# Expert weights in blocks of 896 columns, with a twelve-slot ring and h turned on VectorE

## The chip, the cores and the metric

The kernel runs on one core of one Trainium2 chip. The metric is device time in microseconds for one execution, as the median of several runs. One further execution was recorded by the hardware profiler; the rows below come from it.

## What is computed

One step of a two-layer decoder trunk with model width 1024, for 256 prompt tokens and 8 sample tokens (T = 264), all in 32-bit floats. Layer 0 is an HGRN2 recurrence and a dense SwiGLU, layer 1 a gated short convolution and a mixture of eight experts, of which each token takes two. The change touches the experts alone:

```python
def swiglu(x, w1, w3, w2):
    return (jax.nn.silu(x @ w1) * (x @ w3)) @ w2

def moe_swiglu(x, router, w1, w3, w2):
    logits = (xt @ router).astype(F32)
    top_v, top_i = lax.top_k(logits, TOP_K)
    gates = jax.nn.softmax(top_v, axis=-1)
    ...
    for e in range(N_EXPERTS):
        out = out + combine[:, e:e + 1] * swiglu(xt, w1[e], w3[e], w2[e])
```

w1 and w3 of an expert are 1024 x 3584, w2 is 3584 x 1024. The three together are 44.04 MB per expert and 352.3 MB for the eight.

## The kernel before

**Rows.** The tokens of an expert are gathered into at most 96 rows (`SLOT`), which are three groups of 32 (`GROUPS`, `GROUP`). POOL scatters the normed tokens to `xg_rows` in HBM with indirect DMAs. For each later expert SP loads 96 rows into `xg`, PE turns them (`turn_rows`, L2451), ACT copies them to `xgt` (L1064). The expert's result y is built up in PSUM (`Q[1]`, banks 0 and 1), copied by ACT to `ybuf` and stored to `y_rows`. For the last expert y stays on the chip. Near the end POOL gathers the results of the other experts from `y_rows` (L675).

**Blocks of h.** The 3584 columns of h are worked in FB = 7 blocks of 512. A block has three parts. `up_m(0)` forms x @ w1 of the block, `up_m(1)` forms x @ w3, and `down_m` multiplies h by 512 rows of w2 and adds to y. The stationary operand always is 128 x 32, and four such operands stand side by side in the array, one for each 32 partitions of the output. In `up_m` three of them (L2438) hold the three groups of tokens and see 384 columns (`MAIN`); the fourth (L2442) takes the three groups in turn with the last 128 columns (`TAIL`). In `down_m` the moving operand is 256 columns of w2 for all four (L2500, L2503). Each 32-bit matmul is recorded as two instructions, each with its own weight load.

**Turning h.** ACT forms silu(x @ w1) as `hs` (L1078), DVE multiplies by x @ w3 into `hx` (L1840). Tokens are then on partitions, and `down_m` needs the columns of h there. PE therefore transposes `hx` in three 128 x 128 matmuls (`turn`, L2482) into bank 2 of `Q[0]`, and ACT copies them to `ht` (L1092).

**Order on PE.** One pass of the inner loop is: `up_m(0)` of block i+1, `turn` of block i, `up_m(1)` of block i+1, `down_m` of block i. After six passes the last block of the expert is turned, the rows of the next expert are turned, the last `down_m` runs, both `up_m` of the next expert's first block run, and `clear_y` (L2459, tiny matmuls that start a new y) follows. These stand behind the inner loop as a second copy of the code. The loop over experts goes round seven times, and the last expert has code of its own.

**Loading.** The weights come in pieces of 1 MB (`pair`, `load_piece`, L457): four K tiles of 512 columns of w1 or w3, in rows of 2 KB, or two tiles of w2, in rows of 4 KB. There are 42 pieces per expert and a ring of RING = 6 slots. SP issues the load of a piece when PE has counted (`used`) the piece six places earlier as done. Six pieces are loaded ahead (`early_piece`), the last of them when the normed rows are finished, as its slot holds `gffn` until then.

**Other buffers.** In the stages before the experts, raw weights go to `raw` (three slots of 16 KB a partition) and their split parts to `whi` and `wlo`.

Of the kernel before, what the change touches and what calls it, by code (L numbers as in the profile page):

```python
# [24 lines left out]
P = 128  # L25
# [4 lines left out]
RING = 6  # L30
SLOT = 96
GROUP = 32
MAIN = 384
TAIL = P
# [3 lines left out]
def build(nc, x_prompt, x_sample, state_hgrn, state_conv, norm_mix, norm_ffn, norm_final,  # L38
# [28 lines left out]
    JOB = 3 * FB  # L67
    SLOTS = 3 * SLOT
    GROUPS = SLOT // GROUP
    PIECES = 2 * JOB  # L70
# [3 lines left out]
    assert PIECES % RING == 0 and C_FFN * 2 + 4 == 24 and FW == MAIN + TAIL and D == 4 * YW  # L74
# [4 lines left out]
    with ExitStack() as ctx:  # L79
# [83 lines left out]
        for g_ in range(2):  # L163
# [30 lines left out]
            R0, ("xs", [P, TT, D], F32), ("xgt", [P, DT, SLOT], F32), ("hx", [P, MAIN], F32),  # L194
            ("ht", [P, GROUPS, P], F32), ("sqx", [P, DT, T], F32))
        sqx_at = o - size([P, DT, T], F32)
        (xg, hs), _ = region(sqx_at, ("xg", [P, D], F32), ("hs", [P, MAIN], F32))
# [8 lines left out]
        (ring,), o = region(RING_AT, ("ring", [P, RING, PW], F32))  # L206
        (gffn,), _ = region(RING_AT + (RING - 1) * size([P, PW], F32), ("gffn", [P, D], F32))
# [7 lines left out]
            raw_at + size([P, RAW, CW], F32), ("ht_last", [P, GROUPS, P], F32), ("yh", [P, D], F32R),  # L215
            ("yl", [P, D], F32R), ("pick", [P, T], F32R))
        assert o <= xT_at
# [72 lines left out]
        piece_loaded = [sem(f"piece_loaded{i}") for i in range(RING)]  # L290
        hi_done, lo_done, used = sem("hi_done"), sem("lo_done"), sem("pieces_used")

        OBANK = (0, 1, 3)

# [56 lines left out]
        def _(sp):  # L351
# [102 lines left out]
            def load_piece(q, src):  # L454

                slot = q % RING
                sp.dma_start(ring[:, slot, :].rearrange("p (k w) -> p k w", k=src.shape[1]), src  # L457
                             ).then_inc(piece_loaded[slot], 16)

            def early_piece(q):  # L460

                w = (moe_w1, moe_w1, moe_w3, moe_w3, moe_w1, moe_w1)[q]
                cols = slice(FW, 2 * FW) if q >= 4 else slice(0, FW)
                load_piece(q, tiles_of(w, 0, 4 * (q % 2), 4)[:, :, cols])
# [31 lines left out]
            def head(k, e, row):  # L496

                if not isinstance(k, int):
                    rows_in(k, row)
                    pair(k, 0, tiles_of(moe_w1, e, 0, DT)[:, :, 0:FW])  # L500
                    pair(k, 2, tiles_of(moe_w3, e, 0, DT)[:, :, 0:FW])
                    pair(k, 4, tiles_of(moe_w1, e, 0, DT)[:, :, FW:2 * FW])

            def body(k, e, row, ahead):

                with sp.Fori(0, FB - 2) as i:
                    pair(k, 6, tiles_of(moe_w3, e, 0, DT)[:, :, bass.ds(i * FW + FW, FW)], i)
                    pair(k, 8, tiles_of(moe_w2, e, i * 4, 4), i)
                    pair(k, 10, tiles_of(moe_w1, e, 0, DT)[:, :, bass.ds(i * FW + 2 * FW, FW)], i)
                q = 6 * (FB - 1)  # L510
                if ahead:
                    rows_in(k + 1, row + SLOTS)
                pair(k, q, tiles_of(moe_w3, e, 0, DT)[:, :, FW * (FB - 1):FW * FB])
                pair(k, q + 2, tiles_of(moe_w2, e, 4 * (FB - 2), 4))
                pair(k, q + 4, tiles_of(moe_w2, e, 4 * (FB - 1), 4))
                if ahead:
                    pair(k, q + 6, tiles_of(moe_w1, e + 1, 0, DT)[:, :, 0:FW])
                    pair(k, q + 8, tiles_of(moe_w3, e + 1, 0, DT)[:, :, 0:FW])
                    pair(k, q + 10, tiles_of(moe_w1, e + 1, 0, DT)[:, :, FW:2 * FW])
# [184 lines left out]
        def _(act):  # L704
# [355 lines left out]
            def gathered(k):  # L1060

                act.wait_ge(sem("xg_turned"), k + 2)
                act.wait_ge(used, k * PIECES + (M0 - 4))
# [11 lines left out]
            def silu(nth, last):  # L1075
                act.wait_ge(used, last)
                act.wait_ge(sem("hx_ready"), nth + 1)
                a.activation(hs[:, :], Q[0][:, 0, 0:MAIN], ACT.Silu).then_inc(sem("hs_ready"), 1)  # L1078

            def head(k, e, row):  # L1080
                if not isinstance(k, int):
                    gathered(k)
                silu(k * FB, k * PIECES + (M0 + 2))

            def body(k, e, row, ahead):
                pk = k * PIECES + M0
                kb = k * FB
# [14 lines left out]
                silu(kb + (i + 1), pk + (i * 6 + 6))  # L1102
                turned(kb + i, pk + (i * 6 + 4))
                if ahead:
                    turned(kb + (FB - 1), pk + (6 * FB - 2))
                    gathered(k + 1)
                else:
                    if isinstance(k, int):
# [1489 lines left out]
```

## Time and profile before

| | us |
|---|---|
| median of 3 runs | 1491.7 |
| lowest and highest run | 1490.43, 1495.47 |
| the profiled execution | 1485.0 |
| its span on the core | 1483.2 |
| PE busy in the span | 1453.7 |
| DVE busy, ACT busy | 432.6, 325.1 |
| read from HBM, written | 445.53 MB, 29.66 MB |

The span is the time from the first to the last recorded instruction. Matmuls overlap one another, so the time that PE needs for a piece of work is read from the distance between the starts of matmuls and not from their durations. The experts begin at 541.8 us of the span and their last matmul ends at about 1468 us.

### The profile page before, as it was taken

To read this page: it belongs to the slowest core of one execution; us is meant where nothing else is said; L and a number is where in the kernel's file an instruction comes from. 1 tells how busy PE (TensorE), PEld (TensorE's weight loads), DVE (VectorE), ACT (ScalarE), POOL (GpSimd) and SP (SyncE) were. 2 spreads that over 40 slices of the span, in tenths; PEclk is the share of its full clock that TensorE was granted. 3 is DMA by queue.
4 is the path that set the end of the run, shared out by engine and by line. 5 is a ranking of instruction groups with operands and counts; after the bars stand their busy time and mean duration, and the time that the engine had idled before them with its cause. 6 is when DMAs were issued, how large, how long until landed. Compare 5 with 4: busy or idle time off the path is not lost.

```text
span 1483.2 us, 45976 instructions
## 1 busy us (share of the span) xinstructions
PE 1453.7 (98%) x20875; PEld 1384.1 (93%) x20876; DVE 432.6 (29%) x508; ACT 325.1 (22%) x381; POOL 69.5 (5%) x65
## 2 busy tenths in 40 slices
PE   9998999999999999999999999999999999999996
PEld 8988899999999989999999999999999999999894
DVE  6898866565677620000000000000000000000004
ACT  5644353433353320010010010001001001001012
POOL 1035200000000020000000000000000000001000
PEclk9999999999999999999999999999999999999998
DMA  8645686777648149999999999999999999999994
GB/s 310 220 130 177 221 310 245 268 269 270 232 152 316 40 164 396 392 376 394 396 374 395 394 376 395 393 378 394 394 378 392 396 378 393 394 377 397 388 393 184
DMA packets 214033, 475.95 MB, mean 321 GB/s; under 512 B 8811, under 2 KB 26315, under 8 KB 213981
## 3 DMA queue, kind: packets, MB, share of 16 engines
q1 hardware_dynamic: 210536, 466.47, 86.1%
q10 hardware_dynamic: 2164, 4.40, 0.8%
q0 software_dynamic: 1280, 4.33, 0.8%
q8 instruction: 40, 0.66, 0.2%
q14 instruction: 13, 0.10, 0.0%
HBM read 445.53 MB, written 29.66 MB: 320 GB/s over the span
## 4 chain that ended last, share of the span: by engine, by line
PE 86%; DMA 1%; DVE 1%; ACT 0%; issue 0%; DVEq 0%; SPq 0%
PE Q L2442 25%; PE Q L2438 15%; PE Q L2500 13%; PE Q L1981 8%; PE Q L1982 8%; PE Q L1983 8%; PE Q L2503 7%; PE Q L2482 2%; DMA ring<-in_moe_w 1%; PE Q L2415 0%; PE Q L2451 0%; PE Q L2341 0%; PE Q L2459 0%; PE Q L2369 0%; ACT yrows L1149 0%
## 5 line engine op out<-in xcount | busy, mean ns | idle before, releaser
L2442 PE MATMUL Q<-ring,xgt 128*32 128x128 f32 x5376 | 605.3, 273 | 0.0
L2438 PE MATMUL Q<-ring,xgt 128*32 128x384 f32 x5376 | 597.9, 487 | 0.0
L2442 PEld LDWEIGHTS Q<-ring,xgt 128*32 128x32 f32 x5376 | 582.2, 110 | 0.0
L1981 PE MATMUL Q<-xh,whi 128*128 128x264 f32 x1024 | 294.3, 287 | 5.5 <-DVEq L1285 1.8
L2500 PE MATMUL Q<-ring,ht 128*32 128x256 f32 x3960 | 295.2, 379 | 2.7 <-DMA ring<-in_moe_w 2.2
L2503 PE MATMUL Q<-ring,ht 128*32 128x256 f32 x1320 | 294.5, 379 | 0.0
L1982 PE MATMUL Q<-xl,whi 128*128 128x264 f32 x1024 | 291.7, 285 | 0.0
L1983 PE MATMUL Q<-xh,wlo 128*128 128x264 f32 x1024 | 290.3, 284 | 0.0
L1840 DVE TENSOR_TENSOR hx<-hs,Q 128x384 f32<-128x384 f32 x56 | 31.1, 554 | 883.0 <-PE Q L2442 883.0
L2438 PEld LDWEIGHTS Q<-ring,xgt 128*32 128x32 f32 x5376 | 215.1, 109 | 10.4 <-issue 8.1
L1981 PEld LDWEIGHTS Q<-xh,whi 128*128 128x128 f32 x1024 | 193.3, 189 | 8.2 <-issue 4.2
L1174 DVE TENSOR_TENSOR wlo<-raw,whi 128x2048 fp32r<-128x2048 f32 x77 | 175.8, 2295 | 75.1 <-ACT whi L952 59.5
L1982 PEld LDWEIGHTS Q<-xl,whi 128*128 128x128 f32 x1024 | 193.4, 189 | 0.3
L1983 PEld LDWEIGHTS Q<-xh,wlo 128*128 128x128 f32 x1024 | 193.1, 189 | 0.0
L2500 PEld LDWEIGHTS Q<-ring,ht 128*32 128x32 f32 x3960 | 162.8, 110 | 26.4 <-issue 4.0
L1078 ACT ACTIVATE hs<-Q 128x384 f32<-128x384 f32 x56 | 27.5, 491 | 716.8 <-PE Q L2442 716.8
L2503 PEld LDWEIGHTS Q<-ring,ht 128*32 128x32 f32 x1320 | 144.3, 110 | 0.0
L715 ACT ACTIVATE whi<-raw 128x2048 fp32r<-128x2048 f32 x41 | 78.2, 1912 | 72.0 <-PE Q L1983 71.0
L952 ACT ACTIVATE whi<-raw 128x2048 fp32r<-128x2048 f32 x36 | 68.8, 1911 | 90.2 <-PE Q L1983 90.2
L1983 PE MATMUL Q<-fh,wlo 128*128 128x264 f32 x192 | 54.9, 286 | 0.0
L1982 PE MATMUL Q<-fl,whi 128*128 128x264 f32 x192 | 54.6, 285 | 0.0
L1981 PE MATMUL Q<-fh,whi 128*128 128x264 f32 x192 | 54.4, 283 | 0.0
(282 smaller groups left out, 837.3 us busy)
## 6 DMA issues: line engine op xcount, KB each, us to landing
ring<-in_moe_w SPq DMA_DIRECT2D x336, 1024.0 KB, 9.4
raw<-in_ffn_w SPq DMA_DIRECT2D x42, 1024.0 KB, 6.3
raw<-in_hgrn_w_in SPq DMA_DIRECT2D x16, 1024.0 KB, 6.1
raw<-in_conv_w_in SPq DMA_DIRECT2D x12, 1024.0 KB, 5.8
xg_rows<-zeros SPq DMA_DIRECT2D x6, 1536.0 KB, 9.5
y_rows<-zeros SPq DMA_DIRECT2D x6, 1536.0 KB, 9.6
raw<-in_hgrn_w_out SPq DMA_DIRECT2D x4, 1024.0 KB, 5.1
raw<-in_conv_w_out SPq DMA_DIRECT2D x4, 1024.0 KB, 5.5
```

The source lines that it names most:

```text
L715: a.activation(whi[:, buf, :], raw[:, slot, PW * half:PW * (half + 1)], ACT.Copy).then_inc(hi_done, 1)
L952: a.activation(whi[:, base % SPLIT, :], raw[:, n % RAW, PW * (base % 2):PW * (base % 2 + 1)], ACT.Copy).then_inc(hi_done, 1)
L1174: v.tensor_tensor(low, raw[:, slot, PW * half:PW * (half + 1)], high.bitcast(F32), ALU.subtract).then_inc(lo_done, 1)
L1840: v.tensor_tensor(hx[:, :], hs[:, :], Q[0][:, 1, 0:MAIN], ALU.mult).then_inc(sem("hx_ready"), 1)
L1981: t_.matmul(out, w[wslice], xhi, start=start, stop=False, **kw)
L1982: t_.matmul(out, w[wslice], xlo, start=False, stop=False, **kw)
L1983: return t_.matmul(out, lo[wslice], xhi, start=False, stop=stop, **kw)
L2438: t_.matmul(out[g_, 0:MAIN], xgt[:, kt, g_], w[:, FW * c:FW * c + MAIN], start=(kt == 0), stop=(kt == DT - 1), skip_group_check=True)
L2442: mm = t_.matmul(out[SLOT:P, TAIL * n:TAIL * (n + 1)], xgt[:, kt, g_], w[:, FW * c + MAIN:FW * (c + 1)], start=(kt == 0 and n == 0), stop= ...
L2482: mm = t_.transpose(Q[0][:, 2, P * c:P * (c + 1)], hx[:, P * c:P * (c + 1)], ident[:, :])
L2500: mm = t_.matmul(Q[1][GROUP * n:GROUP * (n + 1), bank, col:col + YW], rows_of_h(ht, f, n), w[:, D * c + YW * cb:D * c + YW * (cb + 1)], st ...
L2503: mm = t_.matmul(Q[1][SLOT:P, bank, col:col + YW], rows_of_h(ht, f, cb), w[:, D * c + 3 * YW:D * (c + 1)], start=False, stop=(last and f = ...
```

## The change

The 3584 columns are worked in MB = 4 blocks of MW = 896. In `up_m` every group of tokens is multiplied by all four column groups at once: four matmuls of HW = 224 columns, one for each 32 partitions of the output. The 224 columns are every fourth run of 32 columns of the block, seven runs 512 bytes apart (`columns`). x @ w1 takes banks 0 and 1 of `Q[0]`, x @ w3 banks 2 and 3. With this layout a transpose of each 32 x 32 block, by one DVE instruction, puts the columns of h on partitions as `down_m` needs them. PE's `turn` and ACT's copy are gone.

The pieces of w1 and w3 are two K tiles of 896 columns (0.875 MB, rows of 3.5 KB), those of w2 two tiles of 128 rows (1 MB), the fourth of a block one tile (0.5 MB): 48 pieces per expert. The ring has twelve slots. Five are where the old ring was, six lie in `raw` and one at the end of `wlo`; the latter seven are loaded when the convolution's output projection is done with that memory. `gffn` has a place of its own.

The code behind the inner loop is gone: the next expert's first `up_m` pair is the last pass of the loop, and `clear_y`, `turn_rows` and one wait stand in the loop under conditions. The diff is cut; of removed lines only some are shown.

```diff
-RING = 6
+RING = 12
+RING_LOW = 5
 SLOT = 96
 GROUP = 32
-MAIN = 384
-TAIL = P
+MW = 896
+HW = MW // 4
...
-        (ring,), o = region(RING_AT, ("ring", [P, RING, PW], F32))
-        (gffn,), _ = region(RING_AT + (RING - 1) * size([P, PW], F32), ("gffn", [P, D], F32))
+        (ring_low, gffn), o = region(RING_AT, ("ring_low", [P, RING_LOW, PW], F32), ("gffn", [P, D], F32))
+        (ring_mid,), o = region(raw_at, ("ring_mid", [P, 2 * RAW, PW], F32))
+        (ring_top,), o = region(xT_at - size([P, PW], F32), ("ring_top", [P, PW], F32))
+        assert RING == RING_LOW + 2 * RAW + 1
...
+        piece_loaded += [raw_loaded[i // 2][i % 2] for i in range(2 * RAW)] + [sem(f"piece_loaded{RING_LOW}")]
+        loaded_before = [C_MOE // RAW if RING_LOW <= i < RING_LOW + 2 * RAW else 0 for i in range(RING)]
...
+        def h_part(which):
+
+            return Q[0][:, 2 * which:2 * which + 2, :].rearrange("p b (h n) -> p (b h) n", n=YW)[:, 0:GROUPS, 0:HW]
...
-            sp.wait_ge(sem("xs_gained"), TT)
-            sp.wait_ge(sem("xs_ready"), TT)
-            early_piece(5)
-
-            def pair(k, q, src, reg=None):
-
-                for half in range(2):
-                    free = k * PIECES + (2 * C_MOE + q + half - RING + 1)
-                    sp.wait_ge(used, free if reg is None else free + reg * 6)
-                    n = src.shape[1] // 2
-                    load_piece(q + half, src[:, n * half:n * (half + 1), :])
+            for i in range(2 * RAW):
+                if i % 2 == 0:
+                    sp.wait_ge(lo_done, 2 * (C_MOE - RAW + i // 2 + 1))
+                early_piece(RING_LOW + i)
+            sp.wait_ge(used, 2 * C_MOE)
+            early_piece(RING - 1)
+
+            def four(k, q, src, reg=None):
+
+                for j in range(4):
+                    free = k * PIECES + (2 * C_MOE + q + j - RING + 1)
+                    sp.wait_ge(used, free if reg is None else free + reg * RING)
+                    load_piece(q + j, src[:, 2 * j:min(2 * j + 2, src.shape[1]), :])
 
...
+                with sp.Fori(0, MB - 2) as i:
+                    four(k, 12, tiles_of(moe_w3, e, 0, DT)[:, :, bass.ds(i * MW + MW, MW)], i)
+                    four(k, 16, tiles_of(moe_w2, e, i * MT, MT), i)
+                    four(k, 20, tiles_of(moe_w1, e, 0, DT)[:, :, bass.ds(i * MW + 2 * MW, MW)], i)
+                q = RING * (MB - 1)
                 if ahead:
                     rows_in(k + 1, row + SLOTS)
+                four(k, q, tiles_of(moe_w3, e, 0, DT)[:, :, MW * (MB - 1):MW * MB])
+                four(k, q + 4, tiles_of(moe_w2, e, MT * (MB - 2), MT))
                 if ahead:
+                    four(k, q + 8, tiles_of(moe_w1, e + 1, 0, DT)[:, :, 0:MW])
+                    four(k, q + 12, tiles_of(moe_w3, e + 1, 0, DT)[:, :, 0:MW])
+                    four(k, q + 16, tiles_of(moe_w2, e, MT * (MB - 1), MT))
+                    four(k, q + 20, tiles_of(moe_w1, e + 1, 0, DT)[:, :, MW:2 * MW])
+                else:
+                    four(k, q + 8, tiles_of(moe_w2, e, MT * (MB - 1), MT))
...
-                def turned(nth, w2_used, ht=ht):
-                    act.wait_ge(sem("h_turned"), nth + 1)
-                    act.wait_ge(used, w2_used)
-                    a.activation(ht[:, :, :].rearrange("p a s -> p (a s)"), Q[0][:, 2, 0:MAIN], ACT.Copy
-                                 ).then_inc(sem("ht_ready"), 1)
-
-                with act.Fori(0, FB - 2) as i:
-                    silu(kb + i + 1, pk + i * 6 + 6)
-                    turned(kb + i, pk + i * 6 + 4)
-                i = FB - 2
...
+            def mul(nth, last, down_before, ht=ht):
                 dve.wait_ge(used, last)
                 dve.wait_ge(sem("hs_ready"), nth + 1)
+                if not isinstance(nth, int) or nth:
+                    dve.wait_ge(sem("ht_ready"), nth)
+                v.tensor_tensor(hx[:, :].rearrange("p (g n) -> p g n", n=HW),
+                                hs[:, :].rearrange("p (g n) -> p g n", n=HW), h_part(1), ALU.mult
                                 ).then_inc(sem("hx_ready"), 1)
+                dve.wait_ge(sem("hx_ready"), nth + 2)
+                if down_before is not None:
+                    dve.wait_ge(used, down_before)
+                v.transpose(ht[:, :], hx[:, :]).then_inc(sem("ht_ready"), 1)
 
...
+            def columns(w, c, n):
+
+                return w[:, MW * c:MW * (c + 1)].rearrange("p (a j r) -> p j a r", j=4, r=GROUP)[:, n, :, :]
+
+            def up_m(which, k, q, reg, first=False):
+
+                for kt in range(DT):
+                    if kt % 2 == 0:
+                        w = piece(k, q + kt // 2, reg)
+                    if first and kt % 4 == 0:
+                        pe.wait_ge(sem("xgt_ready"), kt // 4 + 1)
+                    for g_ in range(GROUPS):
+                        bank, col = 2 * which + g_ // 2, YW * (g_ % 2)
+                        for n in range(4):
+                            mm = t_.matmul(Q[0][GROUP * n:GROUP * (n + 1), bank, col:col + HW],
+                                           xgt[:, kt, GROUP * g_:GROUP * (g_ + 1)], columns(w, kt % 2, n),
+                                           start=(kt == 0 and g_ % 2 == 0), stop=(kt == DT - 1),
+                                           skip_group_check=True)
+                    if kt % 2 == 1:
+                        mm.then_inc(used, 1)
 
...
-                def turn(nth):
-                    pe.wait_ge(sem("hx_ready"), nth + 2)
-
-                    for c in range(GROUPS):
-                        mm = t_.transpose(Q[0][:, 2, P * c:P * (c + 1)], hx[:, P * c:P * (c + 1)],
-                                          ident[:, :])
-                    mm.then_inc(sem("h_turned"), 1)
-
...
+                def down_tile(w, f, cb, last, ht):
+
+                    c = f % 2
+                    bank, col = cb // 2, YW * (cb % 2)
+                    for n in range(GROUPS):
+                        t_.matmul(Q[1][GROUP * n:GROUP * (n + 1), bank, col:col + YW],
+                                  rows_of_h(ht, f, n), w[:, D * c + YW * cb:D * c + YW * (cb + 1)],
+                                  start=False, stop=(last and f == MT - 1), skip_group_check=True)
+                    return t_.matmul(Q[1][SLOT:P, bank, col:col + YW], rows_of_h(ht, f, cb),
+                                     w[:, D * c + 3 * YW:D * (c + 1)],
+                                     start=False, stop=(last and f == MT - 1), skip_group_check=True)
+
...
+                with pe.Fori(0, MB if ahead else MB - 1) as i:
+                    if ahead:
+                        again_if_ahead(i)
                     pe.wait_ge(sem("hs_ready"), kb + i + 1)
+                    up_m(0, k, 8, i)
+                    with pe.If(i == 0):
+                        clear_y(k)
+                    pe.end_ifs()
+                    pe.wait_ge(sem("hx_ready"), kb + i + 2)
+                    up_m(1, k, 12, i)
+                    if ahead:
+                        with pe.If(i == MB - 2):
+                            turn_rows(k + 1)
+                        pe.end_ifs()
+                    down_m(kb + i, 16, i, False)
+                if ahead:
+                    return
```

## Rows read from the trace of the kernel before

**Rows 1.** The page: busy time of PE, and GB/s moved in forty equal slices.
```profile
PE 1453.7 (98%) x20875; PEld 1384.1 (93%) x20876; DVE 432.6 (29%) x508; ACT 325.1 (22%) x381; POOL 69.5 (5%) x65
...
GB/s 310 220 130 177 221 310 245 268 269 270 232 152 316 40 164 396 392 376 394 396 374 395 394 376 395 393 378 394 394 378 392 396 378 393 394 377 397 388 393 184
```

**Rows 2.** Chain that ended last, in order of time: start us, us, what.
```profile
882.02 0.66 PE Q L2451 x8
...
1228.25 0.66 PE Q L2451 x8
...
1267.04 0.48 PE Q L2482 x3
...
1343.66 0.66 PE Q L2451 x8
...
1385.26 0.48 PE Q L2482 x3
```

**Rows 3.** Timeline of PE, one block: start us, us, line, tiles, count.
```profile
904.46 0.55 PE L2482 MATMUL Q<-ident,hx 128*128 128x128 f32 x3
904.94 0.52 PE L2438 MATMUL Q<-ring,xgt 128*32 128x384 f32 x3
...
910.12 0.39 PE L2500 MATMUL Q<-ring,ht 128*32 128x256 f32 x3
...
915.30 0.50 PE L2438 MATMUL Q<-ring,xgt 128*32 128x384 f32 x3
...
920.74 0.55 PE L2482 MATMUL Q<-ident,hx 128*128 128x128 f32 x3
```

**Rows 4.** Timeline of PE at the end of one expert.
```profile
996.88 0.55 PE L2482 MATMUL Q<-ident,hx 128*128 128x128 f32 x3
997.26 0.83 PE L2451 MATMUL Q<-ident,xg 96*128 96x96 f32 x8
998.17 0.42 PE L2500 MATMUL Q<-ring,ht 128*32 128x256 f32 x3
...
1013.96 0.60 PE L2459 MATMUL Q<-ident 32*128 32x1 f32 x4
1014.49 0.52 PE L2438 MATMUL Q<-ring,xgt 128*32 128x384 f32 x3
```

**Rows 5.** Waits of PE: for whom, us in total, times, longest.
```profile
PE Q L2500 <- DMA ring<-in_moe_w: 2.2, 2, 1.8
```

**Rows 6.** Timeline of PE in layer 0, four column groups with 128 columns each.
```profile
115.34 1.08 PE L2084 MATMUL Q<-U,z 128*32 128x128 f32 x32
```

**Rows 7.** Groups by line from 560 to 1460 us: busy us, mean ns of one.
```profile
L1840 DVE TENSOR_TENSOR hx<-hs,Q 128x384 f32<-128x384 f32 x55 | 30.5, 554 | 870.2 <-PE Q L2442 870.2
L1830 DVE SCALAR_TENSOR_TENSOR xs<-xs,tk,xr 128x1024 f32<-128x1024 f32 x2 | 2.6, 1282 | 0.0
```
```profile
L1064 ACT ACTIVATE xgt<-Q 128x768 f32<-128x768 f32 x7 | 5.7, 811 | 1.3 <-PE Q L2451 1.3
```

**Rows 8.** Busy time in stretches; the last three columns are clock, DMA share, GB/s.
```profile
705.00:710.10 5.10, 5.10 (x91) 4.73 (x87) 0.00 (x0) 0.92 (x2) 0.00 (x0) 1.00 1.03 402
...
710.20:715.60 5.40, 5.40 (x107) 5.30 (x103) 0.55 (x1) 0.00 (x0) 0.00 (x0) 1.00 1.05 387
...
900.10:916.40 16.30, 16.30 (x300) 15.79 (x296) 0.56 (x1) 0.91 (x2) 0.00 (x0) 1.00 1.04 394
```

**Rows 9.** Loads at L457 issued in 550 to 560, 1240 to 1250, 1360 to 1370.
```profile
DMA to landing us min/median/max: 9.6/10.2/10.2
```
```profile
DMA to landing us min/median/max: 9.6/10.2/10.3
```
```profile
DMA to landing us min/median/max: 15.5/16.0/16.6
```

**Rows 10.** The page: the queue of instruction loads, and the loads of the ring.
```profile
q8 instruction: 40, 0.66, 0.2%
...
ring<-in_moe_w SPq DMA_DIRECT2D x336, 1024.0 KB, 9.4
```

More of the change, by code:

```diff
@@ L73, in build @@
     CIN_ORDER = [2, 3, 4, 5, 0, 1]
[L74 removed]
+    assert MB * MW == moe_w1.shape[3] and RING == DT + (MT + 1) // 2 and HW <= YW and D == 4 * YW
+    assert C_FFN * 2 + 4 == 24 and C_MOE % RAW == 0
     def kp(w):
@@ L456, in load_piece @@
                 slot = q % RING
[L457 removed]
+                n, w = src.shape[1], src.shape[2]
+                sp.dma_start(ring_slot(slot)[:, 0:n * w].rearrange("p (k w) -> p k w", k=n), src
                              ).then_inc(piece_loaded[slot], 16)
             def early_piece(q):
[L462 to L464 removed]
+                w = (moe_w1, moe_w3, moe_w1)[q // 4]
+                cols = slice(MW, 2 * MW) if q >= 8 else slice(0, MW)
+                load_piece(q, tiles_of(w, 0, 2 * (q % 4), 2)[:, :, cols])
             for c in range(6):
@@ L1135, in body @@
                 act.dma_start(y_rows[bass.ds(row, SLOT), :], ybuf[0:SLOT, :]).then_inc(sem("y_stored"), 16)
-                if ahead:
-                    silu(kb + FB, pk + (6 * FB + 2))
-                else:
+                if not ahead:
                     act.wait_ge(sem("y_stored"), k * 16 + 32)
@@ L2515, in body @@
-                kb = k * FB
-                ends = isinstance(k, int) and not ahead
-                with pe.Fori(0, FB - 2 if ends else FB - 1) as i:
-                    pe.wait_ge(sem("hs_ready"), kb + i + 1)
-                    up_m(0, k, 4, i)
-                    turn(kb + i)
-                    up_m(1, k, 6, i)
-                    down_m(kb + i, 8, i, False)
-                q = 6 * FB - 8
+                def rows_of_h(ht, f, n):
+                    return ht[:, HW * n + GROUP * f:HW * n + GROUP * (f + 1)]
@@ new lines, in down_m @@
+                def down_m(nth, q, reg, last, ends=False, ht=ht):
+                    pe.wait_ge(sem("ht_ready"), nth + 1)
+                    for f in range(4 if ends else MT):
+                        if f % 2 == 0:
+                            w = piece(k, q + f // 2, reg)
+                        for cb in range(GROUPS):
+                            mm = down_tile(w, f, cb, last, ht)
+                        if f % 2 == 1 or f == MT - 1:
+                            mm.then_inc(used, 1)
+                    if ends:
+                        ws = [piece(k, q + j, reg) for j in (2, 3)]
+                        for cb in range(GROUPS):
+                            for f in range(4, MT):
+                                mm = down_tile(ws[f // 2 - 2], f, cb, last, ht)
+                            if cb >= 1:
+                                mm.then_inc(sem("y_mm"), 1)
+                        pe.sem_inc(used, 2)
@@ L2532, in body @@
                         r = rows[t]
-                        mm = t_.transpose(Q[0][:, 3, P * t:P * t + r], pm[0:r, t, :], ident[0:r, 0:r])
+                        mm = t_.transpose(Q[1][:, 3, P * t:P * t + r], pm[0:r, t, :], ident[0:r, 0:r])
                     mm.then_inc(sem("rank_mm"), 1)
-                    down_m(kb + (FB - 2), q + 4, None, False, between=lambda: turn(kb + (FB - 1)))
-                    down_m(kb + (FB - 1), q + 6, None, True, True, None, ht_last)
-                    return
-                turn(kb + (FB - 1))
-                if ahead:
-                    turn_rows(k + 1)
-                down_m(kb + (FB - 1), q + 6, None, True)
-                if ahead:
-                    pe.wait_ge(sem("hs_ready"), kb + FB)
-                    pe.wait_ge(sem("xgt_ready"), k + 3)
-                    up_m(0, k, q + 8, None)
-                    up_m(1, k, q + 10, None)
-                    clear_y(k + 1)
+                down_m(kb + (MB - 1), RING * MB - 4, None, True, ends, ht_last if ends else ht)
             def finish(again):
```

146 lines of the change are left out of this document (49 added, 97 removed).

## The prediction

> **What bounds the kernel now.** I read the page first. PE is busy 98% of the span, and from the fifteenth slice on, where the experts run, the DMA engines move 376 to 397 GB/s in every slice [rows 1]. So two resources look full there, and the question is which of them sets the pace.
>
> The chain of waits says PE: it stays on PE almost everywhere, and consecutive experts follow at the same distance. From 882.02 to 1228.25 us are three experts of 115.41 us each [rows 2]. The one exception is in the last expert. From L2451 of one expert to the second L2482 of the next it is 1267.04 - 1228.25 = 38.79 us, and one expert later, to the turn that stands at the same place, 1385.26 - 1343.66 = 41.60 us [rows 2]. The 2.8 us more are a wait for weights; the waits of PE count 2.2 us of it at L2500 [rows 5].
>
> The timeline of one pass of the inner loop then shows what PE does [rows 3]. The second `up_m` takes 910.12 - 904.94 = 5.18 us, `down_m` 915.30 - 910.12 = 5.18 us, the next `up_m` with the switch to the transposes 920.74 - 915.30 = 5.44 us, and the transposes 904.94 - 904.46 = 0.48 us. Together 16.28 us, of which 0.74 us (0.26 for the change of shape and 0.48) exist only because PE turns h. There is no gap at 915.30, where the loop jumps back.
>
> The DMA is just behind. In a stretch in which mostly 4 KB rows land it moves 402 GB/s, in one of 2 KB rows 387, and over one whole pass 394, always with a DMA share above 1 [rows 8]. A pass needs 6.29 MB, so it costs the DMA 6.29 / 394 = 15.97 us, 0.3 us less than PE takes. The time from issue to landing is 10.2 us at the start of the first expert and again 10.2 us in the seventh [rows 9]. So the DMA never runs dry, and over a whole expert, with the rows loaded and stored, it takes about the same 115.4 us as PE.
>
> **What the ring tolerates.** With six slots a piece is issued when its slot is freed and needed five pieces later: 5 x 115.41 / 42 = 13.7 us. In the last expert, when POOL's gather shares the DMA, landing takes up to 16.6 us [rows 9]. 16.6 - 13.7 = 2.9 us, which is the wait found above. I use the same arithmetic for the new ring.
>
> **The change, part by part.**
>
> *PE's transposes go.* Seven experts lose six turns of 0.74 us in the loop and one at their end, next to `turn_rows`, which still changes the shape; that one costs 997.26 - 996.88 = 0.38 us [rows 4]. 7 x (6 x 0.74 + 0.38) = 33.7 us. The last expert loses seven at 0.74: 5.2 us. Sum -38.9 us, all on the path that sets the end. `turn_rows` (998.17 - 997.26 = 0.91 us) and `clear_y` (0.53 us) stay once per expert and only change place [rows 4].
>
> *The matmuls.* A K tile of 512 columns now takes 5.18 / 8 = 0.648 us, with six matmuls or twelve recorded instructions. 384 columns in half of that is 0.84 ns a column. 256 columns in `down_m` take 5.18 / 24 = 0.216 us, again 0.84 ns a column [rows 3]. Time goes with the columns. Four concurrent matmuls of 224 should then take 0.189 us, a K tile of 896 columns six of these, 1.135 us, and an expert 4 x (96 x 0.189 + 42 x 0.216) = 108.8 us, as now (7 x 15.54 = 108.8). Cost 0. But the instructions come denser. Now there are 96 matmul instructions in 5.18 us, 54 ns for each with its weight load. The change wants one per 1.135 / 24 = 47 ns. No stretch of the experts shows that. Layer 0 does, with the same four column groups in turn: 32 instructions at L2084 last 1.08 us with the last one's 0.27, so 26 ns each [rows 6]. The price is bounded by 0 there and by 54 ns in the experts: 24 x 54 = 1.296 us per K tile, +0.16 us x 512 K tiles = +82 us. I take 0, since L2084 is the nearer form, 32 columns of weights and short runs. The moving operand in runs of 32 columns, 512 bytes apart, is in no row; between 0 and the same +82 us, I take 0.
>
> The Trainium skill (TensorE: Matmul & The Clock Gate, section "Wait — 56ns, not 53.3ns?") says that with hardware decode off the sequencer spends about 62 ns per matmul. By it a K tile would take 24 x 62 = 1.49 us and the kernel would be some 140 us slower in the end; but the 54 ns in [rows 3] and the 26 ns in [rows 6] are both under it, so the trace disagrees.
>
> *DVE and ACT.* The multiply of 384 elements takes 554 ns and one of 1024 takes 1282 ns [rows 7], so 672 take about 0.86 us. The 32 by 32 transpose is not in the trace. It is bounded by nothing below and by two passes over a 1024-element row above, 2.6 us. I take 0.9 us. Either is hidden: the transpose may start when the earlier `down_m` ends, and its result is wanted after both `up_m` of the next block, 18 us later. DVE has nothing else queued but the next multiply. ACT's silu grows to about 0.75 us by the copy of 768 elements in 0.81 [rows 7] and has 9 us; it loses the copy to `ht`. In the last expert `ht_last` is filled 9 us before use. Cost 0.
>
> *The loop.* The jump back shows no gap today [rows 3]. Three conditions per pass are new; if the sequencer runs ahead as it does at the jump, they cost 0. The other bound: the instruction queue loaded 40 packets in 0.2% of 16 engines' span [rows 10], 0.002 x 16 x 1483 / 40 = 1.2 us each. I take 0.
>
> *The DMA.* 512 rows of 2 KB take 1.048 / 387 = 2.71 us, 5.29 ns a row. The 4 KB pieces get the rest of the pass: (15.97 - 4 x 2.71) / 2 = 2.565 us, 10.02 ns a row. A row of 3.5 KB on that line is 10.02 - 4.73 / 4 = 8.84 ns, and a piece of 256 rows 2.263 us. An expert costs 32 x 2.263 + 28 half-MB tiles x 1.283 = 108.3 us, and the row traffic 115.41 - 7 x 15.97 = 3.6 us more, 111.9 us. PE will need 115.41 - 4.82 = 110.6 us. So the DMA becomes the slower of the two, by 1.3 us an expert.
>
> *The ring* decides whether that shows. Twelve slots give 11 x 110.6 / 48 = 25.3 us instead of 13.7. The first seven extra pieces load while the DMA is nearly idle, in the slices with 316, 40 and 164 GB/s [rows 1]. Landing time starts at 10.2 us, grows by 7 x 1.3 = 9.1 and by the gather's 16.0 - 10.2 = 5.8 [rows 9]: 25.1 us. That just fits. The 2.8 us of waiting go, and perhaps 1 us comes back. SP issues 48 pieces instead of 42 per expert and waits for free slots most of the time, so that costs nothing.
>
> **Sum** against the profiled execution: 1485.0 - 38.9 - 2.8 + 1 = 1444.3 us. The median of the runs is 6.7 us above it; I carry that over: 1451 us.
>
> **Rivals.**
>
> *A. As summed, PE sets the pace.* 1441 to 1456 us. Lower end: if the 6.7 us between runs and profile are waits for the DMA, the ring takes them too. Chance 0.58.
>
> *B. The DMA sets the pace.* If 3.5 KB rows are no faster per byte than 2 KB rows, a piece takes 0.875 x 2.71 = 2.371 us and an expert 3.5 us more than above; 7 x 4.8 + 10.2 + 5.8 - 25.3 = 24 us of waits, 1475 us. If each row is cut into 2 KB and 1.5 KB (5.29 + 4.11 ns), a piece takes 2.41 us, the waits 32 us, and the result is 1483 us. If they go like 4 KB rows, 2.244 us, nothing waits. For B speaks that the margin is 0.2 us by my own count; against it, that time per byte falls from 2 to 4 KB rows [rows 8]. Chance 0.24, mostly 1456 to 1483.
>
> *C. PE cannot take instructions that fast*: the other side. The place is `up_m`. The gain of 41 us is gone when a K tile takes 41 / 512 = 0.08 us more than 1.135, which is 50.6 ns per instruction. At today's 54 ns it is +82 us, 1533 us. Against it stand the 26 ns of [rows 6], though over only 32 instructions; for it, that 54 is the fastest any long stretch goes. Chance 0.08.
>
> *D. The longer loop body is fetched anew each pass.* 32 passes with one load of 1.2 us are 38 us, which leaves about 1489 us, no change; with the conditions' jumps too it is slower. Against it: 40 loads in the whole program [rows 10], so neither the inner loop nor the expert loop is reloaded now, and no gap at the jump [rows 3]. The Trainium skill (Runtime: NRT & Kernel Launch, section "Instruction fetch mechanics") states the rule behind this, that a taken branch out of the current two pages stalls on a fetch; the trace does not show such a stall for today's jumps. Chance 0.05.
>
> *E.* 3.5 KB rows are cut into much smaller packets, or the extra early loads delay the last stage before the experts: 0.05, mostly slower.
>
> **How the numbers follow.** A change of 0.3% is what a measurement of this kernel can tell from none. Faster: A, nearly all of B, part of C and D, 0.86. Same: the edge of B and D, 0.03. Slower: 0.11. The range runs from A's low end through most of B: 1440 to 1480. A's own range is 1441 to 1456.
>
> **What would show it.** No L2482; one pass of the loop in 27.2 us, `up_m` 9.08 and `down_m` 9.06 us; L2451 every 110.6 us; PE waits for the ring under 3 us; landing time rising from about 10 to 25 us; 3.5 KB pieces landing every 2.26 us. I am wrong if `up_m` starts are further apart than 47 ns per instruction (C), if PE waits for the ring for tens of us (B), or if a gap stands where a pass begins (D).

## The result and the profile after

The changed kernel takes 1448.6 us (median, 1444.8 to 1449.2), the kernel before 1491.1 us on the same chip: a ratio of 0.9712, 95% interval 0.9695 to 0.9728, so 42.5 us or 2.9% faster. Forecast were 1451 us and a range of 1440 to 1480. The profiled execution took 1449.24 us, with a span of 1447.5 us at a mean granted clock of 0.993.

The page of the kernel after, beside [rows 1 and 10]: busy times, GB/s in forty slices, the queue of instruction loads.
```profile
PE 1419.1 (98%) x22243; PEld 1103.0 (76%) x22244; DVE 458.6 (32%) x516; ACT 296.0 (20%) x301; POOL 68.9 (5%) x65
...
GB/s 314 216 145 183 162 319 219 273 274 275 263 169 289 180 116 381 383 407 408 383 407 409 397 392 409 407 383 408 408 385 407 409 384 407 408 383 407 399 407 178
...
q8 instruction: 41, 0.67, 0.2%
```
From the sixteenth slice on, but for the last, the slices have moved from 374 to 397 GB/s up to 381 to 409. PE is still busy 98% of a span that is 35.7 us shorter, and its matmuls are denser: 22243 where there were 20875. One instruction packet more was loaded.

The chain that ended last, beside [rows 2 to 4]: start, duration, engine, line, count.
```profile
857.51 0.81 PE Q L2470 x8
858.32 0.35 PE Q L2505 x3
867.52 18.16 PE Q L2459 x384
894.75 9.25 PE Q L2459 x192
904.00 0.53 PE Q L2478 x4
904.53 9.22 PE Q L2459 x192
922.81 18.16 PE Q L2459 x384
950.03 18.16 PE Q L2459 x384
968.20 0.81 PE Q L2470 x8
...
1310.33 18.16 PE Q L2459 x384
...
1337.53 3.84 SPq L475
1341.62 2.36 SPq L475
1344.22 22.52 DMA ring_mid<-in_moe_w
1366.78 18.38 PE Q L2459 x384
...
1394.51 18.16 PE Q L2459 x384
```
L2470 is `turn_rows` and stands once per expert; from one to the next it is 110.69 us, where it was 115.41. L2478 is `clear_y`, L2459 `up_m`, L2505 and L2508 are `down_m`, and L475 is SP's instruction that issues a load. Between two starts of L2459 lie 27.22 us (922.81 to 950.03): two `up_m` in 18.16 us and one `down_m` in 9.06. No transposes of h stand there any more, and no gap. In the experts one transfer is on the chain, behind SP's issues, in the last expert; from 1310.33 to 1394.51 us it takes 84.18 us for what takes 82.51 from 867.52 to 950.03, so 1.7 us are lost there.

The waits of PE, beside [rows 5], and DVE's and ACT's operations, beside [rows 7].
```profile
PE Q L2459 <- DMA ring_mid<-in_moe_w: 0.8, 1, 0.8
```
```profile
L1851 DVE TENSOR_TENSOR hx<-hs,Q 128x672 f32<-128x672 f32 x32 | 27.3, 854 | 565.2 <-PE Q L2459 565.2
...
L1100 ACT ACTIVATE hs<-Q 128x672 f32<-128x672 f32 x32 | 23.4, 732 | 610.5 <-PE Q L2459 610.5
L1857 DVE STREAM_TRANSPOSE ht<-hx 128x672 f32<-128x672 f32 x31 | 27.2, 878 | 249.0 <-PE Q L2508 249.0
```
Read from left to right, DVE's new transpose costs 878 ns each and starts when L2508 of `down_m` releases it; nothing on PE waits for either DVE line.

### The profile page after: what moved, and what is told of

Same layout as the page of the kernel before. It is cut to its first block, busy times and chain, and to the rows that moved or that the text cites. A ratio compares the mean times of both kernels' runs of the same rounds, so it can differ in the third digit from the quotient of the medians.

```text
span 1447.5 us, 48564 instructions
## 1 busy us (share of the span) xinstructions
PE 1419.1 (98%) x22243; PEld 1103.0 (76%) x22244; DVE 458.6 (32%) x516; ACT 296.0 (20%) x301; POOL 68.9 (5%) x65
## 4 chain that ended last, share of the span: by engine, by line
PE 84%; DMA 2%; SPq 1%; DVE 1%; ACT 0%; issue 0%; DVEq 0%
PE Q L2459 39%; PE Q L2505 19%; PE Q L1998 8%; PE Q L1999 8%; PE Q L2000 8%; DMA ring_mid<-in_moe_w 2%; SPq L475 1%; PE Q L2508 1%; PE Q L2432 0%; PE Q L2470 0%; PE Q L2358 0%; PE Q L2478 0%; PE Q L2386 0%; ACT yrows L1158 0%; PE Q L2366 0%
## 5 line engine op out<-in xcount | busy, mean ns | idle before, releaser
L2459 PE MATMUL Q<-ring_low,xgt 128*32 128x224 f32 x6192 | 299.2, 353 | 0.0
L2459 PEld LDWEIGHTS Q<-ring_low,xgt 128*32 128x32 f32 x6192 | 202.6, 110 | 88.6 <-DMA ring_low<-in_moe_w 0.4
L2459 PE MATMUL Q<-ring_mid,xgt 128*32 128x224 f32 x4608 | 223.8, 353 | 0.8 <-DMA ring_mid<-in_moe_w 0.8
L2505 PE MATMUL Q<-ring_mid,ht 128*32 128x256 f32 x2790 | 206.8, 379 | 0.2 <-DMA ring_mid<-in_moe_w 0.2
L1851 DVE TENSOR_TENSOR hx<-hs,Q 128x672 f32<-128x672 f32 x32 | 27.3, 854 | 565.2 <-PE Q L2459 565.2
L2508 PE MATMUL Q<-ring_mid,ht 128*32 128x256 f32 x930 | 206.1, 379 | 0.0
L2459 PEld LDWEIGHTS Q<-ring_mid,xgt 128*32 128x32 f32 x4608 | 150.7, 110 | 71.1 <-issue 4.6
L2505 PEld LDWEIGHTS Q<-ring_mid,ht 128*32 128x32 f32 x2790 | 117.0, 110 | 78.4 <-DMA ring_mid<-in_moe_w 1.2
L1100 ACT ACTIVATE hs<-Q 128x672 f32<-128x672 f32 x32 | 23.4, 732 | 610.5 <-PE Q L2459 610.5
L1857 DVE STREAM_TRANSPOSE ht<-hx 128x672 f32<-128x672 f32 x31 | 27.2, 878 | 249.0 <-PE Q L2508 249.0
L2508 PEld LDWEIGHTS Q<-ring_mid,ht 128*32 128x32 f32 x930 | 102.1, 110 | 0.0
L2505 PE MATMUL Q<-ring_low,ht 128*32 128x256 f32 x1116 | 86.4, 380 | 0.3 <-issue 0.2
L2508 PE MATMUL Q<-ring_low,ht 128*32 128x256 f32 x372 | 85.8, 380 | 0.0
## 6 DMA issues: line engine op xcount, KB each, us to landing
ring_mid<-in_moe_w SPq DMA_DIRECT2D x96, 896.0 KB, 14.5
```

The costliest lines, as they stand in the source:

```text
L1100: a.activation(hs[:, :].rearrange("p (g n) -> p g n", n=HW), h_part(0), ACT.Silu).then_inc(sem("hs_ready"), 1)
L1851: v.tensor_tensor(hx[:, :].rearrange("p (g n) -> p g n", n=HW), hs[:, :].rearrange("p (g n) -> p g n", n=HW), h_part(1), ALU.mult).then_in ...
L1857: v.transpose(ht[:, :], hx[:, :]).then_inc(sem("ht_ready"), 1)
L2459: mm = t_.matmul(Q[0][GROUP * n:GROUP * (n + 1), bank, col:col + HW], xgt[:, kt, GROUP * g_:GROUP * (g_ + 1)], columns(w, kt % 2, n), star ...
L2505: t_.matmul(Q[1][GROUP * n:GROUP * (n + 1), bank, col:col + YW], rows_of_h(ht, f, n), w[:, D * c + YW * cb:D * c + YW * (cb + 1)], start=F ...
L2508: return t_.matmul(Q[1][SLOT:P, bank, col:col + YW], rows_of_h(ht, f, cb), w[:, D * c + 3 * YW:D * (c + 1)], start=False, stop=(last and f ...
```

## Experiments

Three theories. **T1** is the prediction's: before, PE and the DMA are level at some 115.5 us per expert, so the change had to relieve both; PE can keep what the transposes gave only because the longer rows and the ring carry the DMA. **T2**: the transposes alone are the gain, rows and ring do nothing. **T3**: the DMA set the pace before and sets it now, the transposes do nothing. Later comes a question on PE's instructions (rivals C and D).

**The transposes away, rows and ring as before** (on the kernel before; h isn't turned, so its products are computed on stale data).
```diff
-                    for c in range(GROUPS):
-                        mm = t_.transpose(Q[0][:, 2, P * c:P * (c + 1)], hx[:, P * c:P * (c + 1)],
-                                          ident[:, :])
-                    mm.then_inc(sem("h_turned"), 1)
+                    pe.sem_inc(sem("h_turned"), 1)
```


> The kernel before, with PE's three transposes of hx left out of every block (the count that ACT waits for is raised directly, so ht holds stale values and the experts' sums are not computed). Three theories. T1, the one of the prediction: before the change PE (115.4 us per expert) and the DMA (about 115.2 us with 2 KB rows) stand level, so taking the transposes off PE alone leaves the DMA as the bound: 3 to 8 us faster than the kernel before, 1483 to 1488 us, L2451 still about 115 us apart, and waits of PE for the ring of 20 to 35 us in all. T2, the transposes alone made the gain and rows and ring are immaterial: about 1450 us, as after the change. T3, the DMA set the pace all along and PE's saving is incidental: within 3 us of the kernel before.

Measured: 1487.3 us, ratio 0.9979 (0.9958 to 0.9999). Some 39 us of PE's work are gone, and at most 0.4% of the time. The waits of PE show where they went:
```profile
PE Q L2438 <- DMA ring<-in_moe_w: 23.3, 20, 3.6
```
In [rows 5] PE's wait for the ring was 2.2 us. L2451 now comes every 116.1 us. The 23.3 us are not all of it: nearly every piece lands just as PE wants it. In one pass the last parts of three pieces land at 1164.72, 1167.43 and 1170.13 us and their first matmuls start at 1164.77, 1167.48 and 1170.18, each some 0.1 us late, which the list of waits doesn't count; these add 0.4 us to a pass. T2 is refuted.

**The transposes put back into the kernel after**, as three idle transposes per pass at the place where the old ones stood.
```diff
+                    for c in range(3):
+                        t_.transpose(Q[1][:, 3, P * c:P * (c + 1)], hx[:, P * c:P * (c + 1)], ident[:, :])
                     up_m(1, k, 12, i)
```


> The changed kernel with three 128 x 128 transposes of hx put back on PE between the two up_m of each of the 31 passes, into a bank that nobody reads; everything else as after the change, so the output is unaffected. T1 and T2: PE sets the pace after the change, so each costs its 0.74 us: +23 us, less the 1.7 us that PE now waits for weights near the end, 1469 to 1472 us. T3 (the DMA sets the pace, PE has slack of its own): under +5 us.

Measured: 1463.2 us, ratio 0.9821 (0.9799 to 0.9844): 14.6 us slower than after. T3, by which it would cost less than 5 us, is refuted. But 14.6 is less than forecast, and the chain says why:
```profile
1267.04 9.08 PE Q L2459 x192
1276.12 0.48 PE Q L2548 x3
1276.59 9.22 PE Q L2459 x192
```
A turn costs 0.48 us itself and makes the next `up_m` 0.14 us longer (9.22 instead of 9.08), 0.62 in all, not 0.74. Next to `clear_y`, in 8 of the 31 turns, that 0.14 is paid already. So 23 x 0.62 + 8 x 0.48 = 18 us, less the 1.7 us that PE otherwise loses in the last expert (below), 16.4. From the first `up_m` to the last matmul of the experts the two profiled executions differ by 904.0 - 888.1 = 15.9 us, the medians by 14.6. (Three transposes of 128 columns turn only 384 of the 672 columns of `hx`: this run prices a stop on PE, it isn't the old method in the new blocks.)

**Rows of 1.75 KB**: each piece of w1 and w3 as two transfers of 448 columns. Bytes, ring and PE's work stay (the counts that PE waits for are doubled to match).
```diff
-                sp.dma_start(ring_slot(slot)[:, 0:n * w].rearrange("p (k w) -> p k w", k=n), src
-                             ).then_inc(piece_loaded[slot], 16)
+                for c in (slice(0, MW // 2), slice(MW // 2, MW)):
+                    sp.dma_start(dst[:, :, c], src[:, :, c]).then_inc(piece_loaded[slot], 16)
```


> The changed kernel with each piece of w1 and w3 loaded by two DMAs, columns 0 to 447 and 448 to 895, so rows of 1.75 KB instead of 3.5 KB; the same bytes, ring and matmuls. T1: a piece costs the DMA 512 x 4.70 ns = 2.41 us instead of 2.26, an expert about 116.6 us, more than PE's 110.7; the ring's slack is used up and PE waits: +28 to +36 us, 1477 to 1485 us. T2: no difference, 1448 us. T3: also about +33 us, so this run tells T2 from the two others.

Measured: 1485.1 us, ratio 0.9963 (0.9947 to 0.9979): 36.5 us slower than after, nearly the whole gain. PE's waits, of which this is the largest line, and the chain:
```profile
PE Q L2464 <- DMA ring_low<-in_moe_w: 12.2, 12, 3.3
```
```profile
951.29 13.07 DMA ring_low<-in_moe_w
...
1068.55 13.02 DMA ring_low<-in_moe_w
```
An expert takes 117.3 us between the same transfer of two experts: the DMA sets the pace, with a DMA share of 1.05 and 384 GB/s over these 117.3 us. Since twice as many transfers are issued as well, row length and the number of transfers are not told apart here.

**Both DMA rates without PE's load**: every second K tile of w1 and w3 left out, once in each kernel (half of those sums isn't computed), so that PE must wait and the DMA shows its own period. For the kernel after; before is cut alike.
```diff
-                    for g_ in range(GROUPS):
+                    for g_ in range(GROUPS if kt % 2 == 0 else 0):
```


> The kernel before, with every second K tile left out of both up_m (so x @ w1 and x @ w3 are summed over half the rows only), all loads kept. PE then needs some 79 us per expert and the DMA alone sets the pace. It measures the DMA's own time per expert with 2 KB rows. T1: 115 to 116 us from one L2451 to the next. T2 (the DMA had room): clearly less, 108 us or below.

> The same cut in the changed kernel: every second K tile left out of both up_m, all loads kept. It measures the DMA's own time per expert with 3.5 KB rows. T1: 32 x 2.263 + 35.9 + 3.6 = 111.9 us per expert, 3.3 us less than with 2 KB rows and 1.2 us more than PE's 110.7. T2: well below 110 us. If 3.5 KB rows had the price of 2 KB rows by the byte: 115 us.

Measured: 1484.1 us with the rows of before, 1445.1 us with those of after (one run each; the uncut kernel before took 1489.1 beside the first). The chain, before cut and after cut:
```profile
1112.11 0.66 PE Q L2451 x8
...
1227.70 0.66 PE Q L2451 x8
```
```profile
954.71 17.10 DMA ring_top<-in_moe_w
...
1066.98 16.93 DMA ring_top<-in_moe_w
```
115.6 us per expert with 2 KB rows, 112.3 with 3.5 KB rows. PE waits 188.9 + 49.9 us for the ring in the first. That is the plainest support for T1: the kernel before without half of its up products is only 5 us faster in its one run, and from its first `up_m` to its last matmul 925.0 us instead of 926.2, because its DMA needed 115.6 us where PE needed 115.41. After, the DMA needs 112.3 and PE 110.7; the same stretch takes 887.0 us with the cut and 888.1 without, and the ratio to before, 1445.1 / 1489.1 = 0.970, can't be told from the 0.971 of the uncut kernel. So the kernel after, too, ends about when the DMA alone would end: the ring, full at the start, lets PE keep its 110.7 us until the last expert. Why the run without transposes came at 116.1 us and not at 115.6 is open.

**The ring's depth**: pieces issued six later, so that only half of the twelve slots are used ahead.
```diff
-                    free = k * PIECES + (2 * C_MOE + q + j - RING + 1)
+                    free = k * PIECES + (2 * C_MOE + q + j - RING + 1 + 6)
```


> The changed kernel, but SP issues a load only when six more pieces have been used than it has to wait for, so at most six of the twelve slots are loading or waiting at a time. T1: the ring then tolerates 5 x 2.31 = 11.5 us of landing time instead of 25.4. With landing at 10.4 us at first and 17 to 24 us later, PE waits for the difference: +10 to +14 us, 1458 to 1463 us, the waits spread over the second to fourth expert and the gather at the end. T2: no difference. T3: no more than +6 us, since a busy DMA stays busy with six slots too.

Measured: 1456.5 us, ratio 0.9789 (0.9757 to 0.9820): 8.0 us slower than after, where 10 to 14 were expected.
```profile
1079.29 0.81 PE Q L2470 x8
...
1191.20 0.81 PE Q L2470 x8
```
These two stand 111.9 us apart and the next one another 112.2, the DMA's own period. The first transfer on this chain starts at 835 us, so until the third expert it still ran at PE's pace. So the deep ring hides a DMA that is 1.3 us per expert too slow; it doesn't make it fast.

**`turn_rows` away too** and with it ACT's copy to `xgt` (the later experts then work on the first one's rows), on the kernel after: 8 transposes fewer in each of seven experts. PE's part of the edit:
```diff
-                for d in range(DT):
-                    mm = t_.transpose(Q[1][:, 2 + d // 4, P * (d % 4):P * (d % 4) + SLOT],
-                                      xg[0:SLOT, P * d:P * (d + 1)], ident[0:SLOT, 0:SLOT])
-                mm.then_inc(sem("xg_turned"), 1)
+                pe.sem_inc(sem("xg_turned"), 1)
```


> The changed kernel with turn_rows left out on PE and the copy to xgt left out on ACT (later experts work on the first expert's rows). PE saves 0.81 + 0.3 us for each of seven experts, 7.7 us in all. T1: PE would need 109.6 us per expert and the DMA 111.9, so the landing time grows by 2.3 us an expert instead of 1.2, reaches the 25 us that the ring bears near the sixth expert, and part is given back: 2 to 5 us faster than the changed kernel, 1444 to 1447 us, with waits of PE for the ring of 4 to 7 us in all. T2 (PE alone sets the time): 1441 us.

Measured: 1452.3 us, ratio 0.9749 (0.9722 to 0.9776), not faster than after (the intervals overlap), where I expected 2 to 5 us of gain. The waits show them given back:
```profile
PE Q L2458 <- DMA ring_low<-in_moe_w: 5.3, 4, 2.2
...
PE Q L2501 <- DMA ring_low<-in_moe_w: 2.4, 1, 2.4
```
With PE at 109.8 us per expert, 0.9 less than after, the ring runs out in the last two experts; the stretch from the last `clear_y` to the last matmul of the experts takes 92.2 us instead of 85.3. So a saving of this kind on PE alone no longer shortens the kernel.

**How fast PE takes instructions.** Rival C priced 47 ns per matmul instruction as the risk. To push further, every matmul of w1 and w3 was cut in two, 128 and 96 columns: the same columns, twice the instructions.
```diff
-                        for n in range(4):
+                        for a0, a1 in ((0, 4), (4, 7)):
+                            for n in range(4):
```


> The changed kernel with each matmul of 224 columns in up_m cut in two, of 128 and 96 columns, with the same operands and result; so 48 instead of 24 recorded matmuls per K tile of 896 columns, each with its weight load. If time goes with the columns and a small fixed part (2.5 ns for each round of four, the difference between 0.1892 us and 224 columns at 2.4 GHz), a K tile takes 1.15 us: +7 to +9 us, 1456 us. If the instruction rate or the 110 ns weight load of a column group is the bound just below today's pace (rival C of the prediction), a K tile takes 48 x 26 ns = 1.25 us (+58 us) or 12 x 0.110 = 1.32 us (+95 us): 1505 to 1545 us.

Measured: 1947.1 us, ratio 1.308 (1.304 to 1.312): 498 us slower than after. Both numbers expected were far off. The page and PE's waits:
```profile
PEclk9999999999999999998989988899889889989998
...
q8 instruction: 338, 5.54, 1.2%
```
```profile
PE Q L2460 <- issue: 328.8, 151, 6.6
```
338 packets of instructions, 16 KB each, instead of 41. The timeline shows PE at full pace between stops:
```profile
976.16 1.33 PE L2460 MATMUL Q<-ring_low,xgt 128*32 128x128 f32 x43
978.62 3.27 PE L2460 MATMUL Q<-ring_low,xgt 128*32 128x96 f32 x128 [1.13 <-issue]
984.57 6.75 PE L2460 MATMUL Q<-ring_low,xgt 128*32 128x96 f32 x211 [2.68 <-issue]
```
128 matmuls in 3.27 us, then nothing for 2.68 us. That looks like rival D, a body fetched anew, not like C. Three kernels tell the two apart. The first has the cut, but drops every second K tile, so the body has as many instructions as after; the second cuts w1 alone, the third K tiles 0 and 4 alone.
```diff
-                    for g_ in range(GROUPS):
+                    for g_ in range(GROUPS if kt % 2 == 0 else 0):
```


> The changed kernel with every matmul of w1 and w3 cut into one of 128 and one of 96 columns, as in i1_twice_the_matmuls, and with every second K tile of these products left out, as in a1_half_k_after (that half of the sums is not computed): the loop body has as many PE instructions as in the changed kernel, and they are as short as in i1. Theory F (i1 lost its time because the longer body was fetched anew in each pass; rival D's mechanism): PE is behind DMA again, 1445 to 1450 us as a1_half_k_after, about 41 packets on the instruction queue, no idle time of PE put down to issue above 10 us, and one call of up_m with its rows at hand takes 4.6 us (half of 9.2). Theory C (PE can't take short matmuls that fast, the prediction's rival C): a call takes half of the 12.3 us that it took in i1, 6.1 us or more, and PE's idle time named issue is 80 us or more here too.


```diff
-                        for a0, a1 in ((0, 4), (4, 7)):
+                        for a0, a1 in ((0, 4), (4, 7)) if which == 0 else ((0, 7),):
```


> The changed kernel with the matmuls of w1 alone cut into 128 and 96 columns. The loop body then has some 1,540 PE instructions (weight loads and matmuls), where the changed kernel has some 1,150 and i1_twice_the_matmuls some 1,920. Theory F: if 1,540 are still held, 1449 to 1455 us and about 41 packets on the instruction queue; if not, the body is fetched anew in each pass, about 6 packets in each of some 47 passes, so 300 packets, and the time is 1650 to 1900 us. Theory C (the rate at which PE takes instructions): half of i1's loss whatever the instruction queue carries, 1690 us, with about 41 packets.


```diff
-                        for a0, a1 in ((0, 4), (4, 7)):
+                        for a0, a1 in ((0, 4), (4, 7)) if kt % 4 == 0 else ((0, 7),):
```


> The changed kernel with the matmuls of K tiles 0 and 4 alone cut into 128 and 96 columns, a quarter of the cuts of i1_twice_the_matmuls; the loop body has some 1,340 PE instructions. Theory F: if that is still held, 1449 to 1452 us with about 41 packets on the instruction queue; if not, some 5 packets in each of 47 passes, about 270 packets, and 1550 to 1800 us. Theory C: a quarter of i1's loss, 1570 us, with about 41 packets.

| kernel | PE instructions in a pass | packets | time, us | ratio to before |
|---|---|---|---|---|
| after | 1,104 | 41 | 1448.6 | 0.971 (0.970 to 0.973) |
| K tiles 0 and 4 cut | 1,296 | 44 | 1456.2 | 0.977 (0.975 to 0.979) |
| w1 cut | 1,488 | 46 | 1470.5 | 0.986 (0.984 to 0.988) |
| all cut, half left out | 1,104 | 41 | 1446.3 | 0.970 (0.968 to 0.972) |
| all cut | 1,872 | 338 | 1947.1 | 1.308 (1.304 to 1.312) |

(Counted are matmul records, each with its weight load: for after two `up_m` of 192 and one `down_m` of 168, twice 552. The expectations took 192 for `down_m`, so their counts are 48 too high.) From the chain of the kernel with w1 cut:
```profile
943.66 18.28 PE Q L2460 x576
```
576 matmuls in 18.28 us where there were 384 in 18.16. The w3 half still takes 9.08, so 384 matmuls of w1 take 9.2 us: 24 ns each with its weight load, in a stretch without idle time. C, which wanted 1690 us for this kernel and 1570 for the one with K tiles 0 and 4 cut, is refuted down to that rate. The Trainium skill (TensorE: Matmul & The Clock Gate, section "Wait — 56ns, not 53.3ns?") gives 62 ns per matmul for the case of hardware decode off. No run shows which setting held here, so the 24 ns say that no such bound was at work; they don't say that the page is wrong, as the prediction's "the trace disagrees" may be read. The loss follows the packets instead: between some 1,490 and 1,870 instructions in the body lies the point from which each pass is fetched anew. With all cut the instruction queue carries ten packets in one pass, from 1006.0 to 1049.5 us, and so on through all 31 passes; in the kernel after it carries none from 620 to 1344 us. Of the 498 us, 328.8 + 33.7 = 362.5 are PE's stops named issue; the lower granted clock (0.937 on average, against 0.993) costs at most some 110 us (an estimate, 0.063 x 1945 less 0.007 x 1448), and how much of that falls into the stops isn't separated.

Theory F of the expectations, a body fetched anew, is right on the packets, but its forecasts for the two partly cut kernels, at most 1455 and 1452 us, are missed by 15 and 4 us, and the kernel with half left out has 12.6 us of stops named issue where at most 10 were expected. The traces show where these stops stand. With w1 cut, five experts in a row take 111.16 us each from `clear_y` to `clear_y`, 0.47 more than after, which is 4 x 0.12 us of longer `up_m`. Its stops named issue (14.5 us) all lie before 590 or after 1365 us, in code that runs for the first time, and in the experts the instruction queue carries packets only up to 612 and after 1365 us; the stops of the kernel with half left out lie between 548 and 580 us. From its first `up_m` to its first `clear_y` the w1 kernel takes 42.5 us, the kernel after 27.4. My reading is that short matmuls outrun the loading of new code; code that is held runs at full pace.

## Why the prediction was right, step by step

- **PE and DMA level before**: right. PE's period 115.41 us, the DMA's own 115.6, measured with PE relieved. (One row was misread without consequence: the full slices in [rows 1] start with the sixteenth, and the lowest is 374 GB/s.)
- **PE's transposes, -38.9 us**: the mechanism is right and for the loop the size too. The forecast was 110.6 us per expert, measured are 110.7. The 0.74 us belong to the old layout, where a change of shape cost 0.26 us; in the new one a turn put back costs 0.62, and 0.48 beside `clear_y`.
- **Matmuls at cost 0**: right. `up_m` 9.08 us (8 x 1.135), `down_m` 9.06. In code that is held, instructions had next to no price down to 24 ns (0.12 us for 192 more of them). The other bound, +82 us, rested on 54 ns as a possible floor; it was only the time of 384 columns.
- **DVE 0.86 and 0.9 us, ACT 0.75**: measured 0.854, 0.878 and 0.732, all hidden. The two rows give 0.88 for the multiply, not 0.86; the 0.9 for the transpose was a guess between wide bounds, and that it fits is luck.
- **The loop**: 0, right, with 41 packets. Rival D was real and only not reached: a body about two thirds longer falls into it, and the price is then not the 38 us that I gave it (one load of 1.2 us in each pass) but 498: 297 packets more, over 31 passes nearly ten in each, and PE stops for them (the 47 passes in two of the expectations are wrong, and so are the five or six packets in each). The Trainium skill (Runtime: NRT & Kernel Launch, section "Instruction fetch mechanics") tells of such a stall on a taken branch out of the current two pages; the 338 packets agree that such a stall exists. The 41 to 46 of the shorter bodies disagree with two pages as its limit here: at 256 instructions to a block of 16 KB (the Trainium skill, same page and section), bodies of 1,104 to 1,488 are longer than two, and they are held.
- **The DMA, 111.9 us per expert**: 111.9 to 112.3 measured, in two kernels in which it sets the pace. Rival B's condition, no gain per byte from 3.5 KB rows, didn't hold. The kernel with 1.75 KB rows is the nearest to what B would have cost: 1485 us, where I had given it 1475 to 1483.
- **The ring, "just fits"**: nearly. Of the 2.8 us of waiting 1.7 remain, where I allowed 1: in the last expert the chain goes through one transfer (22.52 us), where issue itself had fallen behind. The step's account of landing time is wrong, though, see below.
- **The sum**: 1444.3 us for the profiled execution, measured 1449.24, so 4.9 us too low. 2.05 us of that were there at the first expert, already at 400 us, before anything that the change touches; about 0.7 are the last expert's wait, 0.1 per expert over eight 0.8. Of the remaining 1.4 us, 0.7 lie in the first expert, which takes 111.4 us from `clear_y` to `clear_y` instead of 110.7; the rest I can't place. The 2.05 us need not be the change's: with the same code before the experts, two of the kernels above (turns back, half the K tiles) reached their first `up_m` at 541.2 us, after at 543.8 and the one without `turn_rows` at 544.0. **The 6.7 us carried over** from profile to median was the other error, of the opposite sign: the profile before lay below its median, the one after lies 0.7 us above its own. The 1451 owes its closeness to 1448.6 to both.
- **The chances**: A came out. B was near: when PE lost 0.8 us per expert, or the ring half its depth, the DMA set the pace.

## What to carry to other kernels

When PE and the DMA are level, find each one's own period by taking work from the other, and price a change by the larger of the two new periods. Taking 39 us from PE alone gave 4; with longer rows and a deeper ring it gave 42. Cutting matmuls finer costs little in a loop body that is held, 8 to 22 us in code that runs for the first time, and far more once the body no longer fits: 498 us here.

## What I had not expected

Landing time didn't grow to 25 us. Loads at L475 of the kernel after, issued in the ten us from 550 and from 1050 us:
```profile
L475 SPq DMA_DIRECT2D ring_low<-in_moe_w x3: 372/372/373, 551.0 to 555.6; - x3
...
DMA to landing us min/median/max: 10.3/10.4/10.9
```
```profile
L475 SPq DMA_DIRECT2D ring_mid<-in_moe_w x2: 1847/1860/1874, 1057.1 to 1059.7; - x2
...
DMA to landing us min/median/max: 17.2/17.4/17.4
```
It rose to 17 us by 1050 us and stayed there (median 17.0 at 1200, 16.7 at 1240); at the same time the issue instruction itself grew from 0.37 to about 1.86 us. The rest of the lag is therefore, as I read it, in front of the queue, in SP, and a landing time alone understates how late a deep ring is: the time that SP spends in an issue belongs to it. In the last expert, while the gather shares the DMA, an issue takes up to 4.3 us and landing up to 23.9 us. Why the queue takes no more at that point was not tried.

The other surprise is the 498 us above: the same columns and bytes, with a loop body of some 1,870 instructions, ran a third slower.
